# First modulation sums of a hybrid Hyena/attention layer taken as columns, in eight sections loaded in turn with the tokens

## The chip, the cores and the metric

The kernel runs on one core of one Trainium2 chip. The metric is the device time of one execution, in microseconds; lower is better. The engines are PE (matmul), DVE, ACT, POOL and SP (here only a DMA queue).

## The reference, cut to what matters

One diffusion layer over 1024 latent tokens of 1024 channels and 256 context tokens. The change lies in the first step, the modulation of the tokens:

```python
mod_x = (silu(c) @ ada_w[l] + ada_b[l])      # c: (1, 1024), ada_w: (1024, 6144)
mod_c = (silu(c_ctx) @ ada_w[l] + ada_b[l])
sh1, sc1, g1, sh2, sc2, g2 = split(mod_x, 6)
hc = rms(ctx, norm1) * (1 + cc1) + ch1
hx = rms(x, norm1) * (1 + sc1) + sh1
zx = hx @ w_in                                # then Hyena, attention, merge
# the filter network of the Hyena branch, a small MLP over positions
h = sin(fq * (feat @ fw1 + fb1)); h = sin(fq * (h @ fw2 + fb2)); h = sin(fq * (h @ fw3 + fb3))
```

Only sh1 and sc1 (and their context twins ch1, cc1) are needed before the projection: the first 2048 columns of ada_w, 8 MB in f32. All inputs are f32. The rest of the layer (experts, attention) takes most of the time and is not touched.

## The kernel before

The kernel is a sequence of stages, written out by hand: `front`, `attention`, `hyena`, `merge`, `choice`, `experts`. In each, every engine runs its own list in the order of the code, and semaphores tie the lists. No scheduler reorders anything.

The change lies in the first 76 us of `front`. There, five things come together:

- **Constants.** SP loads rows of small vectors, PE transposes them (L754, L755), DVE copies them to cols (L506, L507), ACT makes a sigmoid (L417) and DVE the product sil (L510), 128 x 2 x 8: silu(c) and silu(c_ctx), with the 1024 channels as 8 columns k of 128 partitions.
- **The first modulation sums.** ada holds ada_w's first 2048 columns in four sections of 512 columns (2 MB each). For each section and k, PE takes sil's two columns as weights and the section's 512 columns as moving data (L769), and sums over k into two rows of one of two PSUM banks. ACT copies the rows to SBUF (L462); PE turns the 16 pieces of 2 x 128 to columns of p_mod (L774). A bank is used again only when ACT has copied it.
- **Filter layers.** PE multiplies (L758 and L759 for layer 0, L764 for layer 1, L780 for layer 2), DVE reduces the argument (six operations from L523 to L536), ACT takes the sine (L449). The operands are loaded by ACT's queue; f_in counts their 15 transfers.
- **The tokens.** x_in is loaded in five pieces of 1 MB. ACT squares and sums each tile of 128 tokens (L455), takes the root (L459), DVE inverts it (L797 to L805) and scales the ten tiles (L544).
- **The split.** The projection works on pairs of a high and a low part. For w_raw, ACT makes w_hi (L422) and DVE w_lo (L515). For the tokens, in 24 groups, PE turns four blocks of x_in (L786), DVE and ACT in turn apply shift and scale (hf, L562 and L473), ACT makes h_hi (L478) and DVE h_lo (L569). The first eight groups done, PE starts to project (L221 to L223, three matmuls for each product).

DVE adds the bias to p_mod (L549, L552) behind w_lo of unit 0, and the first hf (L562) needs both. The arrays ada and w_raw have their own buffers, w_raw two. SP issues all large loads in one order: section 0, tokens 0, section 1, tokens 1 and 2, section 2, tokens 3 and 4, section 3, then w_raw of units 0, 1 and 2, the last of which waits for w_lo of unit 0.

Two other places in the program serve for comparison: L716 (column sums of the other modulation parts, 128x128 weights and one moving column) and L1806 (the router in `merge`, 128x128 weights and 16 moving columns).

Of the kernel before, what the change touches and what calls it, by code (L numbers as in the profile page):

```python
# [20 lines left out]
P = 128  # L21
D = 1024
L = 1024
LC = 256
KD = D // P
NT = L // P
NTC = LC // P
NTA = NT + NTC
# [19 lines left out]
FH = 64  # L48
# [18 lines left out]
ACT = mybir.ActivationFunctionType  # L67
AX = mybir.AxisListType.X

UW = 256  # L70
# [63 lines left out]
def build(nc, A, out):  # L134
    root = ExitStack()
    with root:
# [12 lines left out]
        def scope(stack):  # L149
            def sb(name, shape, dt=F32):  # L150
                return stack.enter_context(nc.sbuf_tensor(name, shape, dt))

            def ps(name, shape, dt=F32):
                return stack.enter_context(nc.psum_tensor(name, shape, dt))
            return sb, ps

        g = {"nc": nc, "sem": sem, "scope": scope, "A": A, "out": out}
        sb, _ = scope(root)
# [15 lines left out]
        with ExitStack() as s12:  # L174
            sb12, _ = scope(s12)
            g["qkv"] = sb12("qkv", [P, NTA, QKV])
            g["sil"] = sb12("sil", [P, 2, KD])
            with ExitStack() as s:
                sbh, _ = scope(s)

                with ExitStack() as below:
                    g["ada"] = scope(below)[0]("ada", [P, 2 * D // 512, KD, 512])
                g["h_hi"] = sbh("h_hi", [P, KD, LA], F32R)
                g["h_lo"] = sbh("h_lo", [P, KD, LA], F32R)
                front(g)
            g["tf"] = right.enter_context(nc.sbuf_tensor("dft_in", [P, 10, FC, LQ], F32, side="right"))
            g["decay"] = filters.enter_context(nc.sbuf_tensor("decay_in", [P, NT, HY], F32, side="right"))
            g["fpm"] = filters.enter_context(nc.sbuf_tensor("fpm", [H2, ORD, 2, HY], F32, side="right"))
            attention(g)
            give_back()  # L190
# [35 lines left out]
def front(g):  # L226
# [6 lines left out]
    nc, sem, A = g["nc"], g["sem"], g["A"]  # L233
    ident, ones, cols1, cols2, mod = g["ident"], g["ones"], g["cols1"], g["cols2"], g["mod"]
    h_hi, h_lo, sil, qkv = g["h_hi"], g["h_lo"], g["sil"], g["qkv"]
    GROUPS = [(h, k) for h in range(3) for k in range(KD)]
    SECTIONS = 2 * D // 512
    EARLY = 8
# [18 lines left out]
    with ExitStack() as s:  # L257
# [21 lines left out]
        rows1, rows2 = sb("rows1", [80, P]), sb("rows2", [56, P])  # L279
        sb("rest", [P, 1024])  # L280
        t1 = work[:, 0:L]
# [7 lines left out]
        vec = spare[0:H2, 6144 + 2 * H2:6144 + 2 * H2 + 4]  # L289
        mod_rows = spare[0:2, 3072:3072 + 512 * SECTIONS].rearrange("o (s n) -> o s n", n=512)  # L290
        ada = g["ada"]
        un, kn, hid = spare[0:H2, 5120:5632], spare[0:H2, 5632:6144], g["hid"]
        junk = hf[:].rearrange("p a n -> p (a n)")[:, 0:D]
        p_rows = ps("p_rows", [P, 512])
        p_f = p_g = p_rows
        p_mod = ps("p_mod", [P, 512])
        pz = ps("p_z", [P, BANKS, 512])
        p_sec, p_x = pz[:, 0:2], pz[:, 3:6]
        rows_in, rows2_in = sem("rows_in"), sem("rows2_in")
# [6 lines left out]
        sig_ready, sil_ready = sem("sig_ready"), sem("sil_ready")  # L306
        section_done, section_copied, mod_t = sem("section_done"), sem("section_copied"), sem("mod_t")
        mod_ready = sem("mod_ready")
        ss_ready, root_ready, norm_step, xn_ready = sem("ss_ready"), sem("root_ready"), sem("norm_step"), sem("xn_ready")
# [24 lines left out]
        with nc.Block() as block:  # L334
            @block.sync
            def _(sp):
# [8 lines left out]
                def load_section(i):  # L345
                    sp.dma_start(ada[:, i], A["ada_w"][0][:, 512 * i:512 * i + 512].rearrange("(k p) n -> p k n", p=P))\
                      .then_inc(ada_in[i], 16)

                def load_x(i):
                    src = A["x"][0, 2 * P * i:2 * P * i + 2 * P, :] if 2 * i < NT else A["ctx"][0]  # L350
                    sp.dma_start(x[:, 2 * i:2 * i + 2, :], src.rearrange("(t p) d -> p t d", p=P)).then_inc(x_in[i], 16)

                load_section(0)
                load_x(0)
                load_section(1)
                load_x(1)
                load_x(2)
                load_section(2)
                load_x(3)
                load_x(4)  # L360
                load_section(3)

                def load(u):
                    if u >= 2:
                        sp.wait_ge(w_lo_ready, u - 1)
                    c = unit_column(u)
                    sp.dma_start(w[:, u % 2], A["w_in"][0][:, c:c + UW].rearrange("(k p) n -> p k n", p=P))\
                      .then_inc(w_in[u % 2], 16)
                load(0)
                load(1)  # L370
                load(2)
# [34 lines left out]
            def _(act):  # L406
                act.dma_start(feat, A["feat"]).then_inc(f_in, 16)
                for i, n in enumerate(("filt_b1", "filt_b2", "filt_b3", "filt_freq")):
                    for h in range(2):
                        act.dma_start(vec[FH * h:FH * h + FH, i:i + 1], A[n].rearrange("o h -> h o")).then_inc(f_in, 16)  # L410
                act.wait_ge(f_zero, 2)
                for h in range(2):
                    act.dma_start(w1[:, h, FH * h:FH * h + FH], A["filt_w1"][0]).then_inc(f_in, 16)
                    for t, n in ((w2, "filt_w2"), (w3, "filt_w3")):
                        act.dma_start(t[FH * h:FH * h + FH, FH * h:FH * h + FH], A[n][0]).then_inc(f_in, 16)
                act.wait_ge(cols_ready, 1)
                act.activation(sig[:], cols1[:, 64:80], ACT.Sigmoid).then_inc(sig_ready, 1)  # L417
                def high_part(u):
# [32 lines left out]
                for t in range(NTA):  # L451
                    act.wait_ge(x_in[t // 2], 16)
                    if t:
                        act.wait_ge(ss_ready, t)
                    act.activation(junk, x[:, t, :], ACT.Square, accum_out=ss[:, t:t + 1]).then_inc(ss_ready, 1)  # L455
                    if t == 3:
                        sine(0)
                act.wait_ge(norm_step, 1)
                act.activation(rt[:], ss[:], ACT.Sqrt).then_inc(root_ready, 1)  # L459
                for s_ in range(SECTIONS):  # L460
                    act.wait_ge(section_done, s_ + 1)
                    act.activation(mod_rows[:, s_, :], p_sec[0:2, s_ % 2, :], ACT.Copy).then_inc(section_copied, 1)  # L462
                sine(1)
# [40 lines left out]
            def _(dve):  # L504
# [33 lines left out]
                dve.wait_ge(f_in, 16 * 15)  # L538
                filter_layer(0)
                dve.wait_ge(ss_ready, NTA)  # L540
                dve.tensor_scalar(ss[:], ss[:], 1.0 / D, EPS, ALU.mult, ALU.add).then_inc(norm_step, 1)
                inverse_root(dve, root_ready, norm_step, 1, ss[:], rt[:], r0[:], tt[:])
                for t in range(NTA):
                    dve.tensor_scalar(x[:, t, :], x[:, t, :], r0[:, t:t + 1], None, ALU.mult).then_inc(xn_ready, 1)  # L544
                filter_layer(1)
                weights_low(0)
                dve.wait_ge(mod_t, 1)
                for v in range(2):
# [163 lines left out]
            def _(pe):  # L712
# [42 lines left out]
                pe.transpose(p_rows[:, 80:136], rows2[:], ident[0:56, 0:56]).then_inc(rows_t, 1)  # L755
                pe.wait_ge(f_in, 16 * 15)
                pe.wait_ge(cols_ready, 2)
                pe.matmul(p_f[:], w1[:, 0, :], feat[:, 0:512], start=True, stop=False)  # L758
                pe.matmul(p_f[:], w1[:, 1, :], feat[:, 512:L], start=False, stop=True).then_inc(fz_ready, 1)  # L759
                pe.wait_ge(sil_ready, 1)  # L760
                for s_ in range(SECTIONS):
                    if s_ == 2:
                        pe.wait_ge(sin_ready, 1)
                        pe.matmul(p_f[:], w2, hid[:], start=True, stop=True).then_inc(fz_ready, 1)  # L764
                    pe.wait_ge(ada_in[s_], 16)
                    if s_ >= 2:
                        pe.wait_ge(section_copied, s_ - 1)
                    for k in range(KD):
                        mm = pe.matmul(p_sec[0:2, s_ % 2, :], sil[:, :, k], ada[:, s_, k, :],  # L769
                                       start=k == 0, stop=k == KD - 1)  # L770
                    mm.then_inc(section_done, 1)
                pe.wait_ge(section_copied, SECTIONS)
                for c in range(4 * SECTIONS):
                    mm = pe.transpose(p_mod[:, 2 * c:2 * c + 2], mod_rows[:, c // 4, P * (c % 4):P * (c % 4) + P],  # L774
                                      ident[0:2, 0:2])
                mm.then_inc(mod_t, 1)
                for i, (h, k) in enumerate(GROUPS):
# [1511 lines left out]
```

## Time and profile before

| what | us |
|---|---|
| median of 3 runs | 2298.05 |
| lowest, highest | 2296.43, 2298.7 |
| the profiled execution | 2298.17 |
| its span (first to last instruction) | 2296.3 |
| PE busy in it | 2151.7 |
| DVE busy in it | 1676.6 |
| ACT busy in it | 1139.9 |

The profile gives for each engine its busy time, and the clock that TensorE was granted, as a share of 2.4 GHz. The mean over the execution is 0.97. A line of the timeline is one instruction or several of one kind, merged: start, length, engine, line, output and inputs; a bracket gives the idle time ahead of it and what ended it. A matmul of f32 operands appears as two records, each with its own weight load (PEld).

### The profile page before, as it was taken

What the parts mean: (1) busy time and instruction counts of PE and PEld (TensorE: products, weight loads), DVE (VectorE), ACT (ScalarE), POOL (GpSimd) and SP (SyncE); (2) the same over time, 40 slices, a digit from 0 to 9 for tenths busy, and PEclk for the clock granted to TensorE, in tenths of its full rate; (3) what the DMA queues carried; (4) which work ended last, traced back from release to release, by engine and by line L of the source; (5) the groups of instructions that cost most, each with busy time, mean ns of one, the idle gap of its engine ahead of it and who ended that gap; (6) DMA issues with size and microseconds to landing.
All of it is one profiled execution on the core that took longest, in us unless ns stands there. A gap on an engine that the chain in (4) does not pass through costs nothing.

```text
span 2296.3 us, 27091 instructions
## 1 busy us (share of the span) xinstructions
PE 2151.7 (94%) x10004; PEld 1691.4 (74%) x10004; DVE 1676.6 (73%) x1726; ACT 1139.9 (50%) x1172; POOL 165.2 (7%) x52
## 2 busy tenths in 40 slices
PE   6899999979989999999649999999999999999998
PEld 1898888866658777458538888888888888888886
DVE  2548855147744699555678898888898888898986
ACT  3522121146500211121047777777777777777774
POOL 0000000010000000000000111110111110111100
PEclk9999999989989999999769999999999999999999
DMA  7043445130020213633549999999999999999993
GB/s 279 23 135 119 156 147 193 46 120 15 15 83 1 74 65 138 221 137 134 206 165 342 390 380 378 376 375 390 389 380 379 373 375 390 391 383 376 373 376 110
DMA packets 183082, 539.36 MB, mean 235 GB/s; under 512 B 15151, under 2 KB 57275, under 8 KB 182500
## 3 DMA queue, kind: packets, MB, share of 16 engines
q1 hardware_dynamic: 172704, 506.72, 59.2%
q0 software_dynamic: 4608, 16.78, 2.8%
q10 hardware_dynamic: 5700, 14.90, 1.7%
q8 instruction: 47, 0.77, 0.1%
q14 instruction: 23, 0.19, 0.0%
HBM read 502.71 MB, written 35.65 MB: 234 GB/s over the span
## 4 chain that ended last, share of the span: by engine, by line
PE 47%; ACT 1%; DVE 1%; issue 1%; DMA 0%; POOL 0%; ACTq 0%; POOLq 0%
PE p_a L221 5%; PE p_y L223 5%; PE p_y L221 5%; PE p_a L223 5%; PE p_a L222 5%; PE p_y L222 5%; PE p_b L223 5%; PE p_b L222 5%; PE p_b L221 5%; PE p_t L2214 2%; PE p_t L2205 1%; ACT r_hi L2101 0%; DVE r_lo L2142 0%; DVE au L2172 0%; DMA g1row<-xn_dram,idx_e 0%
## 5 line engine op out<-in xcount | busy, mean ns | idle before, releaser
L2142 DVE TENSOR_TENSOR r_lo<-ring,r_hi 128x2048 fp32r<-128x2048 f32 x384 | 872.0, 2289 | 105.3 <-ACT r_hi L2101 104.9
L2101 ACT ACTIVATE r_hi<-ring 128x2048 fp32r<-128x2048 f32 x384 | 731.7, 1914 | 197.8 <-PE p_b L223 75.3
L221 PE MATMUL p_a<-r_hi,x_hi 128*128 128x512 f32 x512 | 203.5, 398 | 4.3 <-DVE x_lo L2153 4.3
L221 PE MATMUL p_y<-r_hi,a_hi 128*128 128x512 f32 x512 | 205.6, 402 | 0.0
L223 PE MATMUL p_y<-r_hi,a_lo 128*128 128x512 f32 x512 | 200.4, 391 | 0.0
L223 PE MATMUL p_a<-r_hi,x_lo 128*128 128x512 f32 x512 | 200.3, 391 | 0.0
L222 PE MATMUL p_a<-r_lo,x_hi 128*128 128x512 f32 x512 | 200.0, 391 | 0.0
L222 PE MATMUL p_y<-r_lo,a_hi 128*128 128x512 f32 x512 | 199.4, 390 | 0.0
L221 PE MATMUL p_b<-r_hi,x_hi 128*128 128x512 f32 x512 | 199.2, 389 | 0.0
L222 PE MATMUL p_b<-r_lo,x_hi 128*128 128x512 f32 x512 | 199.2, 389 | 0.0
L223 PE MATMUL p_b<-r_hi,x_lo 128*128 128x512 f32 x512 | 199.2, 389 | 0.0
L221 PE MATMUL p_z<-h_hi,w_hi 128*128 128x512 f32 x448 | 177.0, 395 | 0.0
L223 PE MATMUL p_z<-h_hi,w_lo 128*128 128x512 f32 x448 | 174.5, 390 | 0.0
L222 PE MATMUL p_z<-h_lo,w_hi 128*128 128x512 f32 x448 | 174.4, 389 | 0.0
L2076 POOL DMA_INDIRECT g1row<-xn_dram,idx_e x16 | 113.5, 7094 | 57.5 <-DVE idx_e L2148 53.2
L221 PEld LDWEIGHTS p_a<-r_hi,x_hi 128*128 128x128 f32 x512 | 96.7, 189 | 23.7 <-issue 4.6
L223 PEld LDWEIGHTS p_a<-r_hi,x_lo 128*128 128x128 f32 x512 | 96.6, 189 | 20.8
L223 PEld LDWEIGHTS p_y<-r_hi,a_lo 128*128 128x128 f32 x512 | 96.1, 188 | 21.2
L222 PEld LDWEIGHTS p_a<-r_lo,x_hi 128*128 128x128 f32 x512 | 96.8, 189 | 19.2
L223 PEld LDWEIGHTS p_b<-r_hi,x_lo 128*128 128x128 f32 x512 | 96.1, 188 | 19.9
L221 PEld LDWEIGHTS p_b<-r_hi,x_hi 128*128 128x128 f32 x512 | 96.1, 188 | 19.9
L222 PEld LDWEIGHTS p_b<-r_lo,x_hi 128*128 128x128 f32 x512 | 96.1, 188 | 19.9
(298 smaller groups left out, 3514.7 us busy)
## 6 DMA issues: line engine op xcount, KB each, us to landing
ring<-in_w_gate SPq DMA_DIRECT2D x128, 1024.0 KB, 9.1
ring<-in_w_up SPq DMA_DIRECT2D x128, 1024.0 KB, 9.2
ring<-in_w_down SPq DMA_DIRECT2D x128, 1024.0 KB, 12.2
w_raw<-in_w_in SPq DMA_DIRECT2D x17, 1024.0 KB, 6.1
ada_rest<-in_ada_w SPq DMA_DIRECT2D x16, 1024.0 KB, 5.3
ada<-in_ada_w SPq DMA_DIRECT2D x4, 2048.0 KB, 17.2
gate_dram<-zs ACTq DMA_DIRECT2D x16, 512.0 KB, 2.7
x_normed<-gate_dram SPq DMA_DIRECT2D x16, 512.0 KB, 4.3
```

The costliest lines, as they stand in the source:

```text
L221: pe.matmul(out, a_hi, b_hi, start=start, stop=False)
L222: pe.matmul(out, a_hi, b_lo, start=False, stop=False)
L223: return pe.matmul(out, a_lo, b_hi, start=False, stop=stop)
L2076: pool.indirect_dma_start(out=xe[:], out_offset=None, in_=g["xn2_dram"][:, :], in_offset=bass.IndirectOffsetOnAxis(ap=idx_e[:, 0:1], axis=0))\
L2101: act.activation(r_hi[:, i % PARTS], ring[:, i % RAW], ACT.Copy).then_inc(hi_ready, 1)
L2142: dve.tensor_tensor(r_lo[:, i % PARTS], ring[:, i % RAW], r_hi[:, i % PARTS].bitcast(F32), ALU.subtract).then_inc(lo_ready, 1)
L2205: mm = pe.transpose(p_t[:, bank, P * k:P * k + P], xe[:, P * (4 * q + k):P * (4 * q + k) + P], ident[:])
L2214: mm = pe.transpose(p_t[:, q % 2, P * k:P * k + P], au[:, q % 2, P * k:P * k + P], ident[:])
```

## The change

ada has eight sections of 256 columns (1 MB each). For each section, each of its two blocks of 128 columns, and each k, PE takes the 128x128 block of ada as weights and sil's two columns (of c and of c_ctx) as moving data, and sums over k into two columns of p_mod. The rows, ACT's copies and PE's turns are gone; DVE waits for all sections before it adds the bias.

SP loads section 0, tokens 0, section 1, tokens 1, and so on to section 4 and tokens 4, then sections 5 and 6, w_raw of unit 0, section 7, w_raw of units 1 and 2. PE takes filter layer 0 behind section 1 and layer 1 behind section 4 (before: ahead of section 0 and behind section 1). DVE takes the argument of layer 1 ahead of the roots and the scaling of the tokens, not behind. On ACT, the sigmoid comes ahead of 12 of the 15 small loads, the first sine behind six squares instead of four, and the squares' unused output goes to a tile of its own.

```diff
-    SECTIONS = 2 * D // 512
+    SECTIONS = 2 * D // UW
...
-                load_section(0)
-                load_x(0)
-                load_section(1)
-                load_x(1)
-                load_x(2)
-                load_section(2)
-                load_x(3)
-                load_x(4)
-                load_section(3)
...
+                for i in range(NTA // 2):
+                    load_section(i)
+                    load_x(i)
+                load_section(5)
+                load_section(6)
                 load(0)
+                load_section(7)
                 load(1)
...
                 act.dma_start(feat, A["feat"]).then_inc(f_in, 16)
+                act.wait_ge(f_zero, 2)
+                for h in range(2):
+                    act.dma_start(w1[:, h, FH * h:FH * h + FH], A["filt_w1"][0]).then_inc(f_in, 16)
+                act.wait_ge(cols_ready, 1)
+                act.activation(sig[:], cols1[:, 64:80], ACT.Sigmoid).then_inc(sig_ready, 1)
...
-                    if t == 3:
+                    if t == 5:
                         sine(0)
...
-                for s_ in range(SECTIONS):
-                    act.wait_ge(section_done, s_ + 1)
-                    act.activation(mod_rows[:, s_, :], p_sec[0:2, s_ % 2, :], ACT.Copy).then_inc(section_copied, 1)
...
                 filter_layer(0)
+                filter_layer(1)
                 dve.wait_ge(ss_ready, NTA)
...
-                filter_layer(1)
                 weights_low(0)
-                dve.wait_ge(mod_t, 1)
+                dve.wait_ge(sections_done, SECTIONS)
...
                 for s_ in range(SECTIONS):
                     if s_ == 2:
+                        pe.wait_ge(f_in, 16 * 15)
+                        pe.wait_ge(cols_ready, 2)
+                        pe.matmul(p_f[:], w1[:, 0, :], feat[:, 0:512], start=True, stop=False)
+                        pe.matmul(p_f[:], w1[:, 1, :], feat[:, 512:L], start=False, stop=True).then_inc(fz_ready, 1)
+                    if s_ == 5:
                         pe.wait_ge(sin_ready, 1)
                         pe.matmul(p_f[:], w2, hid[:], start=True, stop=True).then_inc(fz_ready, 1)
                     pe.wait_ge(ada_in[s_], 16)
-                    if s_ >= 2:
-                        pe.wait_ge(section_copied, s_ - 1)
-                    for k in range(KD):
-                        mm = pe.matmul(p_sec[0:2, s_ % 2, :], sil[:, :, k], ada[:, s_, k, :],
-                                       start=k == 0, stop=k == KD - 1)
-                    mm.then_inc(section_done, 1)
-                pe.wait_ge(section_copied, SECTIONS)
-                for c in range(4 * SECTIONS):
-                    mm = pe.transpose(p_mod[:, 2 * c:2 * c + 2], mod_rows[:, c // 4, P * (c % 4):P * (c % 4) + P],
-                                      ident[0:2, 0:2])
-                mm.then_inc(mod_t, 1)
+                    for c in range(2):
+                        n = 4 * s_ + 2 * c
+                        for k in range(KD):
+                            mm = pe.matmul(p_mod[:, n:n + 2], ada[:, s_, k, P * c:P * c + P], sil[:, :, k],
+                                           start=k == 0, stop=k == KD - 1)
+                    mm.then_inc(sections_done, 1)
```

On PE, from the constants to the first turned tokens, the kernel before has (p_z stands for the two banks of rows, qkv for the filter's operands that borrow its place, and a row is one matmul or several in a row):

```order
3 L758 MATMUL p_rows<-qkv 128x512
4 L759 MATMUL p_rows<-qkv 128x512
5 L769 MATMUL p_z<-ada,sil 2x512 x16
6 L764 MATMUL p_rows<-hid,qkv 128x512
7 L769 MATMUL p_z<-ada,sil 2x512 x16
8 L774 MATMUL p_mod<-ident,qkv 128x2 x16
9 L786 MATMUL p_z<-ident,x_in 128x128 x24
```

The changed kernel has in the same place:

```order
3 L762 MATMUL p_mod<-sil,ada 128x2 x32
4 L753 MATMUL p_rows<-qkv 128x512
5 L754 MATMUL p_rows<-qkv 128x512
6 L762 MATMUL p_mod<-sil,ada 128x2 x48
7 L757 MATMUL p_rows<-hid,qkv 128x512
8 L762 MATMUL p_mod<-sil,ada 128x2 x48
9 L774 MATMUL p_z<-ident,x_in 128x128 x24
```

32 matmuls of 512 columns and 16 turns became 128 matmuls of two columns, and both filter layers moved behind sections.

On DVE, between the product sil and the first hf, the kernel before has:

```order
9 L536 TENSOR_SCALAR qkv<-qkv 128x512
10 L541 TENSOR_SCALAR ss<-ss 128x10
...
15 L805 TENSOR_TENSOR r<-r,tt 128x10
16 L544 TENSOR_SCALAR x_in<-x_in,r 128x1024 x10
17 L523 TENSOR_SCALAR qkv<-p_rows,qkv 128x512
...
22 L536 TENSOR_SCALAR qkv<-qkv 128x512
23 L515 TENSOR_TENSOR w_lo<-w_raw,w_hi 128x2048
24 L549 TENSOR_TENSOR mod<-p_mod,cols 128x16 x2
```

The changed kernel has there:

```order
9 L528 TENSOR_SCALAR qkv<-qkv 128x512
10 L515 TENSOR_SCALAR qkv<-p_rows,qkv 128x512
...
15 L528 TENSOR_SCALAR qkv<-qkv 128x512
16 L534 TENSOR_SCALAR ss<-ss 128x10
...
21 L793 TENSOR_TENSOR r<-r,tt 128x10
22 L537 TENSOR_SCALAR x_in<-x_in,r 128x1024 x10
23 L507 TENSOR_TENSOR w_lo<-w_raw,w_hi 128x2048
24 L541 TENSOR_TENSOR mod<-p_mod,cols 128x16 x2
```

Filter layer 1 (rows 10 to 15) now stands ahead of the root and the scaled tokens.

## Rows read from the trace of the kernel before

**Rows 1.** The page, parts 1 and 2: PE's busy time, granted clock in tenths.

```profile
PE 2151.7 (94%) x10004; PEld 1691.4 (74%) x10004; DVE 1676.6 (73%) x1726; ACT 1139.9 (50%) x1172; POOL 165.2 (7%) x52
...
PEclk9999999989989999999769999999999999999999
```

**Rows 2.** Timeline, 4 to 76 us: start, length, engine, line, output<-inputs, [idle <-releaser].

```profile
4.04 0.41 SPq L346 DMA_DIRECT2D ada<-in_ada_w  x1
...
6.29 0.24 DVE L506 COPY cols<-p_rows 128x80 f32<-128x80 f32 x1 [6.29 <-PE p_rows L755]
...
10.39 1.28 ACT L417 ACT_TABLE_LOAD   x1 [10.39 <-issue]
...
17.14 2.07 PE L758 MATMUL p_rows<-qkv 33*128 33x512 f32 x2 [10.89 <-DMA qkv<-in_filt_w]
...
20.85 15.20 PE L769 MATMUL p_z<-ada,sil 128*2 128x512 f32 x32
...
24.88 1.24 SPq L346 DMA_DIRECT2D ada<-in_ada_w  x1
...
39.79 0.17 DVE L541 TENSOR_SCALAR ss<-ss 128x10 f32<-128x10 f32 x1 [15.11 <-ACT hf L455]
...
41.90 16.62 PE L769 MATMUL p_z<-ada,sil 128*2 128x512 f32 x32 [4.79 <-ACT qkv L462]
...
49.02 0.80 DVE L523 TENSOR_SCALAR qkv<-p_rows,qkv 128x512 f32<-128x512 f32 x1
...
52.23 0.43 DVE L536 TENSOR_SCALAR qkv<-qkv 128x512 f32<-128x512 f32 x1
...
60.27 1.53 PE L786 MATMUL p_z<-ident,x_in 128*128 128x128 f32 x12
...
62.91 2.29 DVE L515 TENSOR_TENSOR w_lo<-w_raw,w_hi 128x2048 fp32r<-128x2048 f32 x1 [10.26 <-ACT w_hi L422]
...
65.69 0.81 DVE L562 TENSOR_SCALAR hf<-p_z,mod_scale,mod 128x512 f32<-128x512 f32 x1
66.55 1.12 PE L786 MATMUL p_z<-ident,x_in 128*128 128x128 f32 x4 [4.75 <-DVE hf L562]
...
75.76 0.36 PE L221 MATMUL p_z<-w_hi,h_hi 128*128 128x256 f32 x1 [2.15 <-DVE h_lo L569]
```

**Rows 3.** All records of L769: duration in ns, min/median/max.

```profile
L769 PE MATMUL p_z<-ada,sil x64: 592/592/1057, 20.9 to 57.9; 128*2 128x512 f32 x64
```

**Rows 4.** Stretches: length; PE, PEld, DVE, ACT, POOL busy; clock, DMA share, GB/s.

```profile
24.00:37.00 13.00, 13.00 (x31) 2.51 (x28) 0.65 (x2) 8.50 (x13) 0.00 (x0) 1.00 1.03 398
42.00:47.00 5.00, 5.00 (x7) 0.66 (x6) 4.93 (x9) 0.23 (x1) 0.00 (x0) 0.50 1.10 350
```

**Rows 5.** Timeline of L716 and L1806; all of L1806 as in rows 3.

```profile
128.23 0.61 PE L716 MATMUL p_mod<-ones,ada_acc 128*128 128x1 f32 x4 [1.84 <-DVE ada_acc L592]
...
1115.52 3.64 PE L1806 MATMUL p_m<-router_w,h 128*128 128x16 f32 x32
...
L1806 PE MATMUL p_m<-router_w,h x128: 178/263/393, 1045.0 to 1127.3; 128*128 128x16 f32 x128
```

**Rows 6.** Stretches around changes of the granted clock, columns as in rows 4.

```profile
64.40:64.60 0.20, 0.00 (x0) 0.00 (x0) 0.20 (x1) 0.00 (x0) 0.00 (x0) 0.69 0.00 0
...
71.00:71.50 0.50, 0.50 (x3) 0.14 (x2) 0.41 (x2) 0.50 (x2) 0.00 (x0) 0.70 0.00 0
...
1119.00:1119.20 0.20, 0.16 (x2) 0.06 (x1) 0.00 (x0) 0.20 (x1) 0.00 (x0) 0.99 0.50 205
...
1124.00:1127.80 3.80, 3.59 (x16) 3.49 (x16) 2.35 (x9) 0.00 (x0) 0.00 (x0) 0.50 1.01 390
```

**Rows 7.** DMA issues of 4.0, 24.9 and 65.2 us: size, us from issue to landing.

```profile
ada<-in_ada_w SPq DMA_DIRECT2D x1, 2048.0 KB, 9.4
...
ada<-in_ada_w SPq DMA_DIRECT2D x1, 2048.0 KB, 17.9
...
w_raw<-in_w_in SPq DMA_DIRECT2D x1, 1024.0 KB, 5.3
```

More of the change, by code:

```diff
@@ L181, in build @@
                 with ExitStack() as below:
-                    g["ada"] = scope(below)[0]("ada", [P, 2 * D // 512, KD, 512])
+                    g["ada"] = scope(below)[0]("ada", [P, 2 * D // UW, KD, UW])
                 g["h_hi"] = sbh("h_hi", [P, KD, LA], F32R)
@@ L279, in front @@
         rows1, rows2 = sb("rows1", [80, P]), sb("rows2", [56, P])
-        sb("rest", [P, 1024])
+        junk = sb("junk", [P, D])[:]
         t1 = work[:, 0:L]
@@ L289, in front @@
         vec = spare[0:H2, 6144 + 2 * H2:6144 + 2 * H2 + 4]
-        mod_rows = spare[0:2, 3072:3072 + 512 * SECTIONS].rearrange("o (s n) -> o s n", n=512)
         ada = g["ada"]
         un, kn, hid = spare[0:H2, 5120:5632], spare[0:H2, 5632:6144], g["hid"]
-        junk = hf[:].rearrange("p a n -> p (a n)")[:, 0:D]
         p_rows = ps("p_rows", [P, 512])
@@ L297, in front @@
         pz = ps("p_z", [P, BANKS, 512])
-        p_sec, p_x = pz[:, 0:2], pz[:, 3:6]
+        p_x = pz[:, 3:6]
         rows_in, rows2_in = sem("rows_in"), sem("rows2_in")
@@ L306, in front @@
         sig_ready, sil_ready = sem("sig_ready"), sem("sil_ready")
-        section_done, section_copied, mod_t = sem("section_done"), sem("section_copied"), sem("mod_t")
-        mod_ready = sem("mod_ready")
+        sections_done, mod_ready = sem("sections_done"), sem("mod_ready")
         ss_ready, root_ready, norm_step, xn_ready = sem("ss_ready"), sem("root_ready"), sem("norm_step"), sem("xn_ready")
@@ L345, in load_section @@
                 def load_section(i):
-                    sp.dma_start(ada[:, i], A["ada_w"][0][:, 512 * i:512 * i + 512].rearrange("(k p) n -> p k n", p=P))\
+                    sp.dma_start(ada[:, i], A["ada_w"][0][:, UW * i:UW * i + UW].rearrange("(k p) n -> p k n", p=P))\
                       .then_inc(ada_in[i], 16)
@@ L410, in _ @@
                         act.dma_start(vec[FH * h:FH * h + FH, i:i + 1], A[n].rearrange("o h -> h o")).then_inc(f_in, 16)
-                act.wait_ge(f_zero, 2)
                 for h in range(2):
-                    act.dma_start(w1[:, h, FH * h:FH * h + FH], A["filt_w1"][0]).then_inc(f_in, 16)
                     for t, n in ((w2, "filt_w2"), (w3, "filt_w3")):
                         act.dma_start(t[FH * h:FH * h + FH, FH * h:FH * h + FH], A[n][0]).then_inc(f_in, 16)
-                act.wait_ge(cols_ready, 1)
-                act.activation(sig[:], cols1[:, 64:80], ACT.Sigmoid).then_inc(sig_ready, 1)
                 def high_part(u):
@@ L755, in _ @@
                 pe.transpose(p_rows[:, 80:136], rows2[:], ident[0:56, 0:56]).then_inc(rows_t, 1)
[L756 to L759, printed above, removed]
                 pe.wait_ge(sil_ready, 1)
```

## The prediction

> **What bounds the kernel now.** I looked first at the page: PE works for 94% of the span, and the granted clock is at its upper level nearly throughout [rows 1]. After the start, a microsecond taken from any other engine is worth nothing. The change touches only the first 76 us, so I read the timeline of these [rows 2] and asked which wait ends last. The reader is to see a relay. PE transposes the rows of constants, DVE copies them at 6.29, ACT issues its DMAs until 10.39 and only then loads its table for the sigmoid. PE waits for the filter's inputs until 17.14, and sums sections 0 and 1 from 20.85 to 36. Then it is idle, 4.79 us of it up to 41.90 because the bank that it needs is copied by ACT, which stands behind its squares of the tokens and the root. Sections 2 and 3 run from 41.90 to 58.5, the 16 turns follow. ACT goes on to the second sine and w_hi, DVE makes w_lo from 62.91 to 65.20, the sums get their bias, and at **65.69** DVE makes the first hf. From there DVE and ACT set the pace until PE starts to project at 75.76, 10.1 us later; after that PE is the bound. I take 65.69 as the point of comparison: what moves it moves the end by as much, since the code behind it is the same and its loads wait for buffers, not for a time of their own.
>
> **PE's clock in this stretch.** It starts at 1.2 GHz: L758's two records of 512 columns take 2.07 us [rows 2], like the 1057 ns that L769 needs at most, and at 2.4 GHz L769 takes 592 [rows 3]. (The profile prints 1.00 before the first change that it recorded, so the durations decide there.)
>
> **The sums themselves.** Before, a section's 8 matmuls make 16 records of 512 columns on weights two columns wide: about 0.43 us each at full clock (31 records in the 13 us from 24 to 37) [rows 4], some 0.85 at half. After, the order shows 32, 48 and 48 matmuls, 128 in all. Each is two records, as L769's 32 matmuls are 64 records [rows 3], so 256 records, each with its own load of 128x128 weights and two moving columns. The nearest rows are the router's, with the same load and 16 columns [rows 5]. At full clock 32 of them take 3.64 us, and one lasts 0.26: (3.64 - 0.26)/31 = 0.109 us from one to the next. At half clock 16 take 3.59 [rows 6], one 0.39: (3.59 - 0.39)/15 = 0.213. L716, with a single column at full clock, takes 0.61 for four [rows 5], no less for each, so the load sets the price and not the columns. Eight sections of 32 records cost 256 x 0.109 = 27.9 us at full clock and 256 x 0.213 = **54.6 us** at half.
>
> **Which clock.** This decides the sign. The router's 32 records ran from 1115.52 to 1119.16 with PE busy without a gap, and the granted clock fell to 1.2 GHz at 1119.2, in the very moment that they ended [rows 5, 6]. Where PE really idled, from 61.8 (60.27 + 1.53), it was still at full level until 64.5 [rows 2, 6]. So a stream of wide loads with few columns did not hold the clock up, and two columns are fewer still. The router's next 16, at 1124.10, ran at 0.50 from first to last [rows 6]. I take half clock for all eight sections. The streams of 512 columns between them are short: filter layer 0 has 3.7 us (17.14 to 20.85) [rows 2], layer 1 half as many records, so 1.85. After 41.90 the clock was still at 0.50 at 47, after 5.1 us of such records [rows 2, 4], and it rose at 71.3, 4.8 us after 66.55 [rows 2, 6].
>
> The Trainium skill (TensorE: Matmul & The Clock Gate, LDWEIGHTS) gives a weight load as columns / 1.2, in ns, which is 107 ns for 128 columns, with no clock in it. The rows agree at full clock (0.109) and not at half (0.213). By the page's price the sections would cost 27 us and the change would be a gain, as in the first rival.
>
> **When the sections can start and end.** The sigmoid moves ahead of 12 small DMA issues on ACT: cols at 6.5, table load 1.28 [rows 2], two small operations of some 0.2 make sil about 8.5. Section 0 is now 1 MB: not before 4.04 + 5.3 = 9.3 (a megabyte of w_raw in an empty queue), not after the 13.4 at which 2 MB landed (4.04 + 9.4) [rows 7]. I take 10.0, since it is first in the queue. The bytes are the same, in runs of 1 KB and not 2 KB. The loads ran at 398 GB/s while ada and tokens moved and at 350 from 42 to 47, when w_raw's runs of 1 KB did [rows 4]. 8.4 MB at 350 cost 24.0 us for 21.1, and w0 is now ahead of the last section, 3.0 us more: the last section landed at 24.88 + 17.9 = 42.8 [rows 7] and lands now at 48.7. The others land some 6 us apart (1 MB of ada and 1 MB of tokens), faster than the 6.8 in which PE sums one. Loads bind nothing, then. PE's chain is 10.0 + 54.6 + 3.7 + 1.85 = **70.1**. The filter's small inputs are now issued up to about 15.8 (8.5 and 12 issues of 0.6) and were there 6.8 us after the last issue before (10.39 to 17.14), so at 22.6, and PE asks at 10 + 13.7 = 23.7: hidden, by 1 us.
>
> **What lies beside it.** ACT's four copies and PE's 16 turns go, but their place on the chain goes to the sections. DVE now makes filter layer 1 ahead of the roots. It gets the layer at 49.7 and needs 3.6 for it (49.02 to 52.66), 9.2 for the root and ten token tiles (39.79 to 49.02), 2.3 for w_lo [rows 2]: done at 64.8, hidden by the 5.3 us up to 70.1. If the sections were faster this cover would go, and this chain would be late next. Behind the last section PE turns the first four token blocks (before, the first twelve were turned by 61.8, in the shadow of w_lo): 1.1 us, as the four at 66.55 took [rows 2]. The first hf comes at 70.1 + 1.1 = **71.2**, 5.5 us later than 65.69. The profiled execution took 2298.17 with a span of 2296.3. It becomes 2298.17 + 5.5 = **2303.7**; the median of the three runs, 2298.05, lies 0.1 below and changes nothing.
>
> **Rivals.** (1) The other side: the clock rises some 6 us into the stream, since PE has no gap there. The Trainium skill (same page, What's actually happening) sets the clock by how busy PE has been recently, and by that rule a busy PE would be released. Sections then take 3.5 us and wait for their loads. The last ends at 48.7 + 3.5 = 52.2; DVE's chain becomes the bound (layer 1 at 38.5, when section 4 has come, then 3.6 + 9.2 + 2.3 = 53.6), and hf comes at 54.1, behind four small operations of 0.5 in all: 11.6 us earlier, **2286.6**. Two of eight sections at full clock (3.35 each) bring the mark of before back, three make it faster by 0.2%. Against it stand [rows 5, 6]. (2) The filter layers lift the clock for a while behind each: it stayed up 2.7 us after work ended (61.8 to 64.5). 2.7 us at full clock do the work of 5.4, twice, and up to 2.8 by the layers' own halving: up to 8 us, so hf between 63 and 70, about **2299**. Their streams are shorter than those after which it rose here. (3) As forecast, but the clock is still at half when projecting starts, which would be PE's own time. Before, it rose at 71.3, 4.5 us ahead of 75.76, in a stretch of turns and the third layer [rows 2, 6]; the new phase may miss that. From 75.76 PE has no gap, and after 5 us or so of such work it has risen; half of 5.2 is lost: 2.6 on top, **2306.3**.
>
> **How the numbers follow.** Forecast 0.66, at 2303.7, its own range 2301 to 2306.5 (section 0 from 9.3 to 11, inputs 1 us late, turns hidden or not). Rival 1 0.11, rival 2 0.11, rival 3 0.12. 0.2% (4.6 us), about what a measurement of this kernel can tell from no change, puts the upper bound at 2302.65, close below the forecast. Slower: three quarters of 0.66 and all of rival 3, 0.62. Faster, below 2293.5: rival 1 and 0.02 of rival 2, 0.13. The same: 0.25. The range 2296.5 to 2308 leaves out rival 1, a third of rival 2 and a little above.
>
> **What would show it.** Right: records of the new line 0.21 us apart, granted clock 0.50 from the start to past 70, PE busy from 10 to 70 without waiting for ada, first hf near 71, DVE's w_lo done before the last section. Wrong: records 0.11 apart with waits for loads between sections (rival 1), a clock that goes up behind L753 or L757 (rival 2), or a last section that lands later than 63.

## The result, and the profile after

The changed kernel takes 2305.25 us (median of 7 runs, 2303.12 to 2305.5), the kernel before 2297.75 in the same measurement (7 runs, 2296.43 to 2298.7). The ratio is 1.003, 95% interval [1.0019, 1.0042]: slower by 0.3%, some 7 us. The forecast was 2303.7, with 2296.5 to 2308. The profiled execution, 2303.12 with a span of 2301.2, is the quickest of the seven. Of all executions counted in this document one was disturbed (3981.13 us at a mean granted clock of 0.76): it is left out of its median, and its profile is not read.

The timeline of the changed kernel, 9 to 82 us (start, length, engine, line, output<-inputs, idle time ahead and what ended it):

```profile
9.11 6.96 PE L762 MATMUL p_mod<-sil,ada 128*128 128x2 f32 x32 [3.02 <-DMA ada<-in_ada_w]
...
16.65 6.98 PE L762 MATMUL p_mod<-sil,ada 128*128 128x2 f32 x32 [0.58 <-DMA ada<-in_ada_w]
...
27.27 20.64 PE L762 MATMUL p_mod<-sil,ada 128*128 128x2 f32 x96
...
47.77 2.05 PE L757 MATMUL p_rows<-hid,qkv 128*128 128x512 f32 x2
...
49.61 20.48 PE L762 MATMUL p_mod<-sil,ada 128*128 128x2 f32 x96
...
61.57 2.29 DVE L507 TENSOR_TENSOR w_lo<-w_raw,w_hi 128x2048 fp32r<-128x2048 f32 x1
...
69.95 4.90 PE L774 MATMUL p_z<-ident,x_in 128*128 128x128 f32 x24
...
71.16 0.81 DVE L554 TENSOR_SCALAR hf<-p_z,mod_scale,mod 128x512 f32<-128x512 f32 x1 [0.50 <-PE p_z L774]
...
81.23 0.36 PE L221 MATMUL p_z<-w_hi,h_hi 128*128 128x256 f32 x1 [2.15 <-DVE h_lo L561]
```

Where [rows 2] had PE idle to 17.14 and again up to 41.90, PE now starts its sums at 9.11 and has one gap of 0.58 us until 69.95. That early start does not bring the end of the sums forward: DVE's w_lo is finished at 63.9, and DVE then waits 6.28 us for PE. The first hf comes at 71.16 instead of 65.69, and the first projection at 81.23 instead of 75.76, both 5.47 us later.

All records of the new line together (ns, min/median/max), of which there are 256:

```profile
L762 PEld LDWEIGHTS p_mod<-sil,ada x256: 285/333/337, 9.1 to 69.7; 128*128 128x128 f32 x128
L762 PE MATMUL p_mod<-sil,ada x256: 213/353/371, 9.1 to 69.7; 128*128 128x2 f32 x128
```

The load lasts 333 ns in the median and not less than 285 anywhere. At the upper clock such a load lasts about 190 (runs below). 96 records in 20.64 us, the last of them 0.35, are 0.2136 from one to the next: half clock from the first to the last. (Three sections are 96 records, two for each of 48 matmuls.)

Loads in two stretches (PE, PEld, DVE, ACT, POOL busy; clock, DMA share, GB/s), and the issue of the last section (at 36.77):

```profile
24.00:37.00 13.00, 13.00 (x50) 10.45 (x49) 3.47 (x6) 6.50 (x11) 0.00 (x0) 1.00 1.07 374
37.00:47.00 10.00, 10.00 (x49) 10.00 (x48) 0.00 (x0) 3.48 (x5) 0.00 (x0) 1.00 1.10 348
```

```profile
ada<-in_ada_w SPq DMA_DIRECT2D x1, 1024.0 KB, 12.2
```

In [rows 4] the first of these stretches ran at 398 GB/s. The smaller runs cost about what was reckoned (348 in the second stretch, 350 in the prediction), and the last section is there at 49.0 (36.77 + 12.2), 14 us before PE asks for it.

### The profile page after: what moved, and what is told of

It reads as the page before. It is cut to its first block and busy times, and to the rows that moved or that the text cites. A ratio compares the mean times of both kernels' runs of the same rounds, so it can differ in the third digit from the quotient of the medians.

```text
span 2301.2 us, 27441 instructions
## 1 busy us (share of the span) xinstructions
PE 2171.7 (94%) x10180; PEld 1738.6 (76%) x10180; DVE 1676.5 (73%) x1726; ACT 1137.4 (49%) x1168; POOL 165.2 (7%) x52
## 5 line engine op out<-in xcount | busy, mean ns | idle before, releaser
L223 PEld LDWEIGHTS p_a<-r_hi,x_lo 128*128 128x128 f32 x512 | 96.6, 189 | 20.7
```

The costliest lines, as they stand in the source:

```text
L223: return pe.matmul(out, a_lo, b_hi, start=False, stop=stop)
```

## The experiments

Times stand beside those of the kernel before on the same chip: 2296.92 for the first four, 2296.46 for the next four, 2296.43 for the two that follow and 2295.93 for the last one.

### The changed kernel again

No edit.

> The changed kernel unchanged, for a second profile of it. Theory A (weight loads at half clock): the first hf again within 0.5 us of 71.2, records of the new line 0.213 us apart; time 2303 to 2305.5. The seven times already known fall in two bunches, near 2303.3 and near 2305.3. If this run is of the upper bunch, theory A with rival 3 says that the clock is still at 0.5 for some microseconds behind 81.2, where projecting starts; if the clock there is full, the 2 us lie in some later stage, where the stretches at 0.5 are longer than in the first profile.

2303.66 (8 runs, 2301.5 to 2304.48), ratio 1.0029 [1.0018, 1.004]. The first hf came at 71.28. The profiled execution took 2303.25, and around the first projection it differs from the first profile (timeline, then stretches of 1, 1 and 3 us):

```profile
81.35 0.55 PE L221 MATMUL p_z<-w_hi,h_hi 128*128 128x256 f32 x1 [2.15 <-DVE h_lo L561]
```

```profile
79.00:80.00 1.00, 0.20 (x2) 0.00 (x0) 0.91 (x3) 0.97 (x3) 0.00 (x0) 1.00 0.00 0
80.00:81.00 1.00, 0.00 (x0) 0.00 (x0) 1.00 (x2) 0.85 (x2) 0.00 (x0) 0.63 0.00 0
81.00:84.00 3.00, 2.65 (x12) 2.68 (x13) 2.86 (x6) 1.56 (x3) 0.00 (x0) 0.50 0.01 3
```

The clock fell at 80.3, in the idle 2.15 us ahead of the projection, and its first records came at half clock (0.55 for 0.36). So rival 3 of the prediction does happen, in some executions: the clock fell a second time, rather than failing to rise. The expectation had tied such a fall to the slower bunch of executions, near 2305.3; this execution, at 2303.25, belongs to the quick one. Where the 2 us between the bunches lie was not found.

### Columns alone, on the kernel before

```diff
-                    for k in range(KD):
-                        mm = pe.matmul(p_sec[0:2, s_ % 2, :], sil[:, :, k], ada[:, s_, k, :], ...)
-                    mm.then_inc(section_done, 1)
+                    for c in range(4):
+                        n = 8 * s_ + 2 * c
+                        for k in range(KD):
+                            mm = pe.matmul(p_mod[:, n:n + 2], ada[:, s_, k, P * c:P * c + P], sil[:, :, k], ...)
+                    mm.then_inc(sections_done, 1)
```

> The kernel before with nothing but the sums taken as columns: four sections of 512 columns, the old order of loads, filter layers and sigmoid. Theory A (the price is 256 weight loads at half clock): sections 0 and 1 run from 20.85 to 48.2, filter layer 1 to 50.0, sections 2 and 3 to 77.3, first hf at 78.4, which is 12.7 us later than before: 2310. Rival B (the columns are cheap, and the loss came from smaller loads or from the new order): 0.11 us per record, sections end at 50, first hf near 54, 2286.

2309.96 (4 runs, 2309.03 to 2310.95), ratio 1.0055 [1.0039, 1.0072]: 13 us slower than before. Its timeline:

```profile
20.48 27.47 PE L766 MATMUL p_mod<-sil,ada 128*128 128x2 f32 x128
...
49.66 27.31 PE L766 MATMUL p_mod<-sil,ada 128*128 128x2 f32 x128
...
78.03 0.81 DVE L559 TENSOR_SCALAR hf<-p_z,mod_scale,mod 128x512 f32<-128x512 f32 x1 [0.49 <-PE p_z L778]
```

The first hf was expected at 78.4 and came at 78.03. Rival B, that the columns are cheap, is out: alone they cost twice what the whole change costs. The rest of the change, which lets PE start at 9.1 instead of 20.5 but puts filter layer 0 among the sums, gives 6 us of it back.

### 128 moving columns

```diff
+                dve.tensor_copy(silw.rearrange("p k (r s) -> p s k r", s=2),
+                                sil[:].unsqueeze(3).broadcast_to([P, 2, KD, WIDE // 2]))
...
-                            mm = pe.matmul(p_mod[:, n:n + 2], ada[:, s_, k, P * c:P * c + P], sil[:, :, k],
+                            mm = pe.matmul(to, ada[:, s_, k, P * c:P * c + P], silw[:, k, :],
```

Each block of ada now has a piece `to` of 128 PSUM columns, in p_mod and three banks of p_z, and DVE adds the bias to columns 0 and 1 of each. The matmuls compute 126 columns that nobody uses.

> The changed kernel with one thing different: sil's two columns are repeated to 128 moving columns (one small DVE copy), so that the same 256 weight loads each carry 128 columns, of which two are used. Theory A (few moving columns keep the clock down): it rises some 5 us into the stream and stays, records come 0.11 us apart, PE then waits for each section's load, and DVE's chain sets the first hf at 54 to 56: 2286 to 2289, 10 us faster than before. Rival C (wide weight loads themselves keep the clock down, whatever moves): nothing changes, 2304 to 2306. Rival D (128 columns do not fit beside the load): at full clock 0.22 us per record, sections end near 70 again, 2304.

2288.53 (5 runs, 2285.53 to 2289.8), ratio 0.996 [0.9946, 0.9974]: 8.4 us faster than before, and 15.1 faster than the changed kernel with 256 identical weight loads. Its timeline:

```profile
9.16 5.24 PE L770 MATMUL p_mod<-qkv,ada 128*128 128x128 f32 x32 [3.07 <-DMA ada<-in_ada_w]
...
17.30 3.84 PE L770 MATMUL p_mod<-qkv,ada 128*128 128x128 f32 x32 [2.89 <-DMA ada<-in_ada_w]
...
40.07 7.41 PE L770 MATMUL p_z<-qkv,ada 128*128 128x128 f32 x64 [0.89 <-DMA ada<-in_ada_w]
...
50.51 6.70 PE L770 MATMUL p_z<-qkv,ada 128*128 128x128 f32 x32 [3.03 <-DMA ada<-in_ada_w]
...
57.95 0.81 DVE L561 TENSOR_SCALAR hf<-p_z,mod_scale,mod 128x512 f32<-128x512 f32 x1
```

The clock rose within the first section (5.24 us for 32 records, neither 7.0 nor 3.8). From the second on, 32 records take 3.84, (3.84 - 0.27)/31 = 0.115 each, and PE waits for loads, as rival 1 had pictured. The moving columns fit beside the weight load, so rival D is out, and so is C. The first hf was expected at 54 to 56 and came at 57.95. What spoils it is the last section. PE had nothing to do for 3.03 us, and the clock fell, at 49.7:

```profile
47.00:48.00 1.00, 0.48 (x5) 0.29 (x3) 1.00 (x3) 0.98 (x1) 0.00 (x0) 1.00 1.12 354
49.00:50.00 1.00, 0.00 (x0) 0.00 (x0) 1.00 (x3) 0.00 (x0) 0.00 (x0) 0.86 0.53 181
50.00:51.00 1.00, 0.49 (x2) 0.49 (x3) 1.00 (x3) 0.00 (x0) 0.00 (x0) 0.50 0.31 109
```

### 64 and 32 moving columns

The same edit with WIDE = 64 and WIDE = 32.

> As the run with 128 moving columns, with sil repeated to 64. It looks for the point at which the clock lets go, with the same 256 weight loads. Theory A (what moves decides): 0.11 us per record once it has risen; if it rises and stays, first hf at 54 to 58, 2286 to 2290; if 64 are too few, 0.213 per record throughout and 2304 like the changed kernel. I expect that it rises. Theory C (loads alone decide) is out already.

> The same with 32 moving columns. Theory A: too few, since the router's 16 let the clock fall in the trace of before; records 0.213 us apart all the way, first hf near 71, 2303 to 2306. If it rises here, hf is at 54 to 60.

One run of each: 2294.19 and 2302.9. Records of 64 columns (p_mod are sections 0 to 3, p_z 4 to 7), and the three sections behind filter layer 1:

```profile
L770 PEld LDWEIGHTS p_mod<-qkv,ada x128: 287/333/338, 9.2 to 41.1; 128*128 128x128 f32 x128
...
L770 PEld LDWEIGHTS p_z<-qkv,ada x128: 191/192/337, 41.3 to 60.9; 128*128 128x128 f32 x128
```

```profile
48.25 2.02 PE L764 MATMUL p_rows<-hid,qkv 128*128 128x512 f32 x2
50.07 11.18 PE L770 MATMUL p_z<-qkv,ada 128*128 128x64 f32 x96
...
64.92 0.81 DVE L561 TENSOR_SCALAR hf<-p_z,mod_scale,mod 128x512 f32<-128x512 f32 x1
```

Records of 32 columns:

```profile
L768 PEld LDWEIGHTS p_mod<-qkv,ada x256: 285/333/337, 9.1 to 69.8; 128*128 128x128 f32 x128
```

I expected 64 to rise at once, and they did not: half clock from 9 to 48, through five sections. Behind filter layer 1 (two records of 512 columns) the clock went up and stayed, and 96 records took 11.18 us (20.48 in the changed kernel). The sums were done at 61.3, and yet the first hf came only at 64.92: filter layer 1 had still been made at half clock, and DVE's chain behind it (layer 1, root, tokens, w_lo until 64.3) ended last. With 32 the loads lasted 333 ns (the median; 285 at least) to the end and the first hf came at 71.30, as with two columns. This run has the same copy of sil and the same kind of moving operand as the one with 128, and section 0, in which the clock rose there, goes to p_mod in both; so none of these lifted the clock, and the number of moving columns is what is left. In these profiles the clock never rose with 2 or 32 columns, with 64 only behind the wider records of filter layer 1, and with 128 within five microseconds. For 32 and 64 that is one execution each, and that it was the wider records that lifted the clock at 64 is read from the time at which it rose, not tested.

### Rows in the new order

```diff
+                    for k in range(KD):
+                        mm = pe.matmul(pz[0:2, s_ // 2, UW * (s_ % 2):UW * (s_ % 2) + UW], sil[:, :, k], ada[:, s_, k, :],
+                                       start=k == 0, stop=k == KD - 1)
+                    mm.then_inc(section_done, 1)
+                for c in range(16):
+                    if c in (0, 12):
+                        pe.wait_ge(section_copied, 3 + c // 12)
+                    mm = pe.transpose(p_mod[:, 2 * c:2 * c + 2], mod_rows[:, c // 4, P * (c % 4):P * (c % 4) + P],
+                                      ident[0:2, 0:2])
...
+                for q in range(3):
+                    copy_pair(q)
                 sine(1)
                 high_part(0)
+                copy_pair(3)
```

> The changed kernel's loads and order, with the sums taken as rows again (sil as weights of two columns, 256 moving columns, 8 sections; ACT copies pairs of sections, the last pair behind w_hi; 16 turns). Theory A: half clock for the first 6 us or so, then 0.215 us per record, 3.5 us per section, the loads of the sections bind, last section lands near 49, first hf at 54 to 55: 2287. Rival B (the loss came from loads or order): the first hf stays near 70, about 2304.

2287.67 (4 runs, 2284.76 to 2289.24), ratio 0.9955 [0.9938, 0.9972]. Its timeline:

```profile
9.31 6.37 PE L767 MATMUL p_z<-ada,sil 128*2 128x256 f32 x16 [3.27 <-DMA ada<-in_ada_w]
...
16.85 3.62 PE L767 MATMUL p_z<-ada,sil 128*2 128x256 f32 x16 [1.16 <-DMA ada<-in_ada_w]
...
49.28 3.62 PE L767 MATMUL p_z<-ada,sil 128*2 128x256 f32 x16 [1.96 <-DMA ada<-in_ada_w]
...
54.68 0.81 DVE L561 TENSOR_SCALAR hf<-p_z,mod_scale,mod 128x512 f32<-128x512 f32 x1
```

ACT's copies and PE's 16 turns are back with the rows. This is the changed kernel without its first idea, and it is 16 us faster than with it. Loads, order, sigmoid and filter layers of the change are a gain of 9 us; the columns turn that into a loss. A section of rows takes 3.62 us at full clock, about what one of columns takes there (3.84 with 128 columns). Rows are hardly cheaper; what they have ahead of two columns is that the clock rises under them, within the first section (6.37 us, then 3.62).

### Holding the clock through the idle stretch ahead of projecting

```diff
                     mm.then_inc(x_t, 1)
+                    if i == KD + 1:
+                        for _ in range(2):
+                            pe.matmul(p_mod[:], ident[:], x[:, 0, 0:512], start=True, stop=True)
                     if i > KD and i % 2:
```

> The changed kernel with two matmuls of 512 columns, whose result nobody reads, on PE in the idle 2.15 us ahead of the first projection. In one of its two profiles the clock fell there (at 80.6) and the first projection records came 0.213 us apart for 5 us; in the other it did not. Theory (rival 3: part of the spread and of the loss is the clock at the start of projecting): the clock stays up in every run, first projection near 81.3, time 0 to 2 us below the changed kernel, 2301.5 to 2303.7. Rival: the added matmuls delay the project start by some tenths and nothing is gained, 2303.7 to 2304.5.

> The kernel with rows in the new order, and the same two matmuls ahead of the first projection. Its own profile had the clock fall at 66, 1.3 us into projecting. Theory: the clock stays up, PE gains 2 to 3 us: 2285 against 2287.7. Rival (the fall is not caused by the idle stretch): unchanged, 2287.7.

On the changed kernel 2301.4 (7 runs, 2298.44 to 2303.92), ratio 1.0027 [1.0015, 1.0039]; without the two matmuls 2303.66, ratio 1.0029 [1.0018, 1.004]. On the kernel with rows 2284.09 (seven runs from 2281.96 to 2284.97 and one of 2294.2), ratio 0.995 [0.9937, 0.9963]; without them 2287.67, ratio 0.9955 [0.9938, 0.9972]. The medians are 2.3 and 3.6 lower, and that is what was expected, but the intervals overlap widely in both pairs: a gain is likely, and not shown. The two timelines (changed kernel, then rows):

```profile
79.17 1.88 PE L778 MATMUL p_mod<-x_in,ident 128*128 128x512 f32 x4
...
81.49 0.36 PE L221 MATMUL p_z<-w_hi,h_hi 128*128 128x256 f32 x1 [0.44 <-DVE h_lo L561]
```

```profile
62.44 1.88 PE L789 MATMUL p_mod<-x_in,ident 128*128 128x512 f32 x4
...
64.76 0.36 PE L221 MATMUL p_z<-w_hi,h_hi 128*128 128x256 f32 x1 [0.44 <-DVE h_lo L568]
```

Four records without use took 1.88 us of an idle stretch, the projection started where it did without them, at full clock. In the eight profiles of this study without them (the kernel before not counted), the projection starts at half clock in three (again, columns alone, 128 columns), the clock falls 1.4 and 1.0 us behind its first record in two (rows, and the last run below), and it stays up in three (the first profile, 64 and 32 columns). In the three profiles with them (these two and the run below with filter layer 1 earlier) it stays up.

What a fall there is worth at the end is less than it looks. Line L708 of the changed kernel (L716 before the change), which comes again and again while PE projects, serves as a milestone. Its records up to 280 us, with first and last start, and below them the stretch from 134 to 142, each time for the first profile, the second one and the one with the two matmuls:

```profile
L708 PE MATMUL p_mod<-ones,ada_acc x28: 164/250/272, 132.9 to 278.1; 128*128 128x1 f32 x28
L708 PE MATMUL p_mod<-ones,ada_acc x28: 164/250/271, 134.9 to 278.9; 128*128 128x1 f32 x28
L708 PE MATMUL p_mod<-ones,ada_acc x28: 164/250/272, 132.5 to 275.0; 128*128 128x1 f32 x28
```

```profile
134.00:142.00 8.00, 6.91 (x35) 6.91 (x36) 4.64 (x9) 0.44 (x2) 0.00 (x0) 0.57 0.81 261
134.00:142.00 8.00, 6.01 (x37) 5.73 (x36) 4.73 (x7) 2.51 (x3) 0.00 (x0) 0.79 0.79 253
134.00:142.00 8.00, 7.31 (x61) 7.31 (x62) 4.78 (x10) 1.10 (x3) 0.00 (x0) 1.00 0.78 255
```

The second execution, whose clock fell at 80.3, is 2.0 us behind the first at 133, but only 0.8 at 278: in between, the first one had the clock at half for longer (a mean of 0.57 for 0.79 in these 8 us). At the end they differ by 0.13 (2303.25 and 2303.12). The execution with the two matmuls is 0.4 ahead of the first at 133 and 3.1 at 278, and its clock did not fall near 134 at all (1.00); both projected at full clock. So most of the 4.7 us between these two executions (2298.44 and 2303.12) does not come from the start of projecting, where the two matmuls stand.

### The idle stretch ahead of the last section

```diff
                         pe.matmul(p_f[:], w2, hid[:], start=True, stop=True).then_inc(fz_ready, 1)
+                    if s_ == 7:
+                        for _ in range(2):
+                            pe.matmul(pz[:, 5], ident[:], ada[:, 0, 0:2, :].rearrange("p k n -> p (k n)"), ...)
                     pe.wait_ge(ada_in[s_], 16)
```

This is an edit of the kernel with 128 moving columns.

> The kernel with 128 moving columns, and two matmuls of 512 columns (result unused) on PE between sections 6 and 7. Without them PE had nothing to do from 47.5 to 50.5, the clock fell at 50, and the last section took 6.7 us instead of 3.8 (first hf at 57.95). Theory (an idle stretch costs the clock, and the last section's 3 us are its price): the last section takes 3.8, first hf at 55, 2285.5. Rival (the last section is slow for another reason, such as the load of w_raw beside it): 6.7 us again, 2288.5.

> The same kernel as the last one with 128 moving columns, for a profile (the one taken shows a disturbed execution). Its undisturbed times, 2286.9 to 2288.9, are 1 us below those without the two matmuls, where 3 were expected. If the idle stretch was the cause, the last section takes 3.8 us here, first hf at 55, and the missing 2 us lie elsewhere, at the start of projecting, where the clock fell in the run without them. If not, 6.7 us again and hf at 58.

2287.06 (5 runs, 2286.9 to 2288.85), ratio 0.9962 [0.9948, 0.9976], and again 2286.97 (4 runs, 2285 to 2289), ratio 0.9963 [0.9943, 0.9982]. The second one's timeline:

```profile
47.07 1.88 PE L767 MATMUL p_z<-ada,ident 128*128 128x512 f32 x4
49.76 3.84 PE L773 MATMUL p_z<-qkv,ada 128*128 128x128 f32 x32 [0.81 <-DMA ada<-in_ada_w]
...
54.33 0.81 DVE L561 TENSOR_SCALAR hf<-p_z,mod_scale,mod 128x512 f32<-128x512 f32 x1
```

The last section takes 3.84 us and not 6.70, and hf comes at 54.33 and not at 57.95, the place that the prediction's first rival had worked out (54.1). The mechanism is shown: w_raw's loads were as before, and filling the wait was enough. The gain in time is not: 2285.5 was expected, the medians are 1.5 lower than the 2288.53 without, and the ratios are the same (0.9962 and 0.9963 for 0.996). In this profile the clock fell at the start of projecting instead, at 65.4, 1.0 us behind the first record.

### Filter layer 1 one section earlier

On the kernel with rows and the two matmuls ahead of projecting:

```diff
-                    if s_ == 5:
+                    if s_ == 4:
```

> Rows in the new order with the two matmuls ahead of projecting, and filter layer 1 behind section 3 instead of 4, so that DVE's chain (layer 1, root, tokens, w_lo) is done some 3 us sooner, near 49.5. In the run without this, w_lo ended at 52.66, the last section at 52.9, and the turns at 54.0. Theory (after w_lo the last section's load binds, ending at 49): first hf at 54.4 to 54.7 as before, since ACT's copy of the last pair and the turns follow the last section: no gain over 2284.1, within 1 us. Rival (DVE's chain still binds): hf 1 us or more sooner, 2283.

2283.89 (4 runs, 2282.15 to 2286.07), ratio 0.9943 [0.9926, 0.9959], against 2284.09 without: no gain, as expected. DVE's w_lo ended 2.8 us sooner (50.69 for 53.46) and nobody was waiting for it:

```profile
48.40 2.29 DVE L514 TENSOR_TENSOR w_lo<-w_raw,w_hi 128x2048 fp32r<-128x2048 f32 x1
```

The last section in this profile took 5.30 us and not 3.62, since the clock fell at 48.9, at the end of the 2.02 us in which PE waited for it; the first hf came at 55.91, where 54.4 to 54.7 was expected. An execution in which it does not fall was not profiled. Both kernels, at 2284, are the fastest of this study, 12 us under the kernel before.

## Why the prediction was right

**The price of a record.** Taken at 0.213 us from the router's records at half clock [rows 5, 6], measured 0.2136. Eight sections were put at 54.6 us; four pieces of timeline (6.96, 6.98, 20.64, 20.48) give 55.1, less the overlap of records at their seams.

**The clock.** This was the step that set the sign, and it rested on one place of the trace: the clock that fell while PE was busy with the router's narrow records [rows 5, 6]. The loads of 333 ns up to 69.7 bear it out, and the runs with 128 and with 32 columns show the cause: they differ in the number of moving columns, and only the first one's clock rose. The prediction inferred from 16 columns in another stage to two here; the 32 columns bear that out. The filter layers, with 3.7 and 1.85 us of wider records, did not lift the clock in any of the three profiles with two columns in the new order (rival 2), but with 64 it rose behind the second of them.

**The rules that were weighed.** The traces have a 128-column weight load spaced 0.109 to 0.115 us apart at the upper level and 0.213 at the lower. From the formula of the Trainium skill (TensorE: Matmul & The Clock Gate, LDWEIGHTS), columns / 1.2, a load of 128 columns is estimated at 107 ns. The trace agrees at the upper level only. In the changed kernel PE is busy by the profile for 60 us with one gap of 0.58 and stays at 1.2 GHz. The Trainium skill (TensorE: Matmul & The Clock Gate, What's actually happening) lets the clock follow how busy PE has been recently. By the trace, being busy in the profile's sense is not what counts.

**Start and loads.** Section 0 was there at 9.0, not 10.0, and the sums started at 9.11; that is 0.9 in the change's favour. The wait of 0.58 us for section 1, where the prediction had none, and some tenths elsewhere took it back. The filter's inputs, put at 22.6, were there at 20.7 in the run with rows, so they were hidden by more than reckoned. PE came to the turned tokens at 69.95 (70.1 predicted), the last section landed at 49.0 (48.7), w_lo ended at 63.9 (64.8), hf came at 71.16 (71.2).

**From hf to the end.** The sum moved the end by as much as hf, 5.5 us. The profiled execution has 5.47 at the projection and 4.9 at the end of the span, the medians 7.5 and 6.7 in two measurements. The step that was a little short is this one: "what moves it moves the end by as much". Behind hf there are idle stretches of 2 us, where the clock falls in one execution and not in another. Rival 3 with its 2.6 us had a chance of 0.12. One of two profiles shows its half clock, and the median of 2305.25 lies between the forecast and rival 3. But this does not make rival 3 the cause of the missing 1.6 us: the execution with the fall took 0.13 more than the one without, since the clock was at half elsewhere for longer in the other. What separates 2303 from 2305 stays open.

**The range.** It held the time, and its low end, drawn for rival 2, was not needed. That the forecast lies within 1.6 us of the median is in part luck: executions of this kernel spread over 2.4 us and more, and a second measurement gave 2303.66.

## What to carry to other kernels

Turning a matmul so that the wide operand becomes the weights does not save PE time by itself: in f32, a 128x128 block of the matrix took about as long as weights as its 128 columns took as moving data on narrow weights, here 3.84 for 3.62 us per section at full clock. It also takes away the moving columns under which TensorE's clock had risen, and at half clock a section takes 6.9 us. Where a stretch at the start of a kernel binds, look at the clock's level, from the durations, before counting instructions; feeding a stream that is bound by its weight loads with columns that nobody uses cost next to nothing here and brought 15 us. Filling an idle wait with a wide matmul kept the clock up in every profile and delayed what follows by 0.3 us at most, but its gain in time was not shown. Parts of a change that come together should be run apart: here a gain of 9 us was hidden in a loss of 7.

## What the runs showed of the hardware that I had not expected

- The same 256 loads of 128x128 f32 weights: with 2 or 32 moving columns the clock never rose in 60 us; with 64 it did not for 39 us, rose behind two records of 512 columns, and stayed up to the end of the sums; with 128 it rose within 5 us.
- 128 moving columns beside a load of 128x128 f32 weights cost at most 0.006 us (0.115 from one record to the next, for 0.109 with the router's 16), and 64 cost the same 0.115.
- An idle stretch of 2 to 3 us lowered the clock in some executions and not in others, at the same place of the same kernel (80.3 in one profile of the changed kernel, not at all there in the other). Two executions can differ in where the clock falls and still end 0.13 us apart; how much of the spread of 2 us and more comes from it was not worked out.
